# The weights of an input projection: eleven more units split into two matmul parts, with all thirteen low parts of that pass made by GpSimd

## The reference

```
mod = silu(c) @ w_ada + b_ada                     # six vectors per sequence
h = rmsnorm(x) * (1 + sc1) + sh1
proj = h @ w_in                                   # 1024 -> 2176 columns: 17 units of 128
ya = pool_mixer(proj[..., :256]);  yb = conformer_conv(proj[..., 256:1024]);  yc = short_conv(proj[..., 1024:])
x = x + gt1 * rmsnorm(concat(ya, yb, yc) @ w_out)
h = rmsnorm(x) * (1 + sc2) + sh2
x = x + gt2 * rmsnorm((silu(h @ w_gate) * (h @ w_up)) @ w_down)
```

## Time and profile before

| | |
|---|---|
| median of 3 runs | 2261.96 us (2261.28 to 2262.41) |
| profiled execution, its own time | 2261.27 us |
| its span | 2259.5 us |
| granted TensorE clock, mean | 0.999 |
| busy: PE, DVE, ACT, POOL | 2244.3, 1343.5, 1001.7, 38.1 us |

### The profile page before, as it was taken

One profiled execution on the slowest core, in us unless ns is written; L12 is line 12 of the kernel. 1 busy time (PEld: TensorE's weight loads), 2 busy tenths in 40 slices (PEclk: granted clock), 3 DMA queues, 4 the chain that ended last, 5 costly groups with the idle time before them and its releaser, 6 DMA issues.

```text
span 2259.5 us, 29953 instructions
## 1 busy us (share of the span) xinstructions
PE 2244.3 (99%) x12270; PEld 2069.7 (92%) x12270; DVE 1343.5 (59%) x1957; ACT 1001.7 (44%) x1408; POOL 38.1 (2%) x83
## 2 busy tenths in 40 slices
PE   9999999999999999999999999999999999999998
PEld 6779998979999988999898899989899998899987
DVE  3779866698444577653467855357784435443343
ACT  3455466454444534353544435354443425432332
POOL 0000000000000000000000000000000000000000
PEclk9999999999999999999999999999999999999999
DMA  9864653544443533544353353435335434444332
GB/s 376 309 221 164 242 200 137 177 168 169 167 151 129 183 125 123 185 149 156 125 185 123 126 210 122 156 124 186 122 128 180 123 130 153 155 149 159 123 129 94
DMA packets 103046, 368.98 MB, mean 163 GB/s; under 512 B 12631, under 2 KB 14807, under 8 KB 102396
## 3 DMA queue, kind: packets, MB, share of 16 engines
q1 hardware_dynamic: 102910, 367.06, 45.8%
HBM read 348.02 MB, written 19.00 MB: 162 GB/s over the span
## 4 chain that ended last, share of the span: by engine, by line
PE 91%; DVE 4%; ACT 0%; issue 0%; DMA 0%; DVEq 0%; ACTq 0%
PE ps L636 90%; DVE wlo L1349 1%; DVE pr L1500 1%; PE ps L706 1%; DVE early L1500 0%; PE ps L666 0%; DVE g_lo L1401 0%; DMA raw<-in_w_mix 0%; DVE h_lo L1394 0%; ACT h_f L1035 0%; ACT junk L990 0%; DVE pr L1522 0%; DVE h_wait L1378 0%; ACT whi L967 0%; DVE h_wait L1380 0%
## 5 line engine op out<-in xcount | busy, mean ns | idle before, releaser
L1349 DVE TENSOR_TENSOR wlo<-raw,whi 128x1024 fp32r<-128x1024 f32 x531 | 646.7, 1221 | 525.6 <-ACT whi L967 524.1
L636 PE MATMUL ps<-h_hi,whi 128*128 128x384 f32 (+1 forms) x2808 | 923.9, 329 | 1.9 <-DVE h_lo L1394 1.1
L967 ACT ACTIVATE whi<-raw 128x1024 fp32r<-128x1024 f32 x531 | 561.1, 1058 | 817.8 <-DMA raw<-in_w_gu 536.9
L636 PE MATMUL ps<-h_hi,wlo 128*128 128x384 f32 (+1 forms) x2808 | 919.4, 327 | 0.0
L636 PE MATMUL ps<-h_lo,whi 128*128 128x384 f32 (+1 forms) x2808 | 919.2, 327 | 0.0
L636 PEld LDWEIGHTS ps<-h_hi,whi 128*128 128x128 f32 x2808 | 528.6, 188 | 8.4 <-issue 4.8
L636 PEld LDWEIGHTS ps<-h_lo,whi 128*128 128x128 f32 x2808 | 528.6, 188 | 1.8
L636 PEld LDWEIGHTS ps<-h_hi,wlo 128*128 128x128 f32 x2808 | 528.6, 188 | 0.0
L636 PE MATMUL ps<-whi,g_hi 128*128 128x512 f32 x748 | 235.1, 395 | 1.7 <-issue 0.9
L636 PE MATMUL ps<-whi,g_lo 128*128 128x512 f32 x748 | 231.1, 390 | 0.0
L636 PE MATMUL ps<-wlo,g_hi 128*128 128x512 f32 x748 | 230.8, 390 | 0.0
(11 more groups left out here) (143 smaller groups left out, 1303.7 us busy)
## 6 DMA issues: line engine op xcount, KB each, us to landing
raw<-in_w_gu SPq DMA_DIRECT2D x264, 512.0 KB, 3.2
raw<-in_w_mix SPq DMA_DIRECT2D x150, 512.0 KB, 3.2
raw<-in_w_dn SPq DMA_DIRECT2D x132, 512.0 KB, 3.2
xr<-in_x_all SPq DMA_DIRECT2D x29, 512.0 KB, 5.9
xr<-x_all SPq DMA_DIRECT2D x17, 512.0 KB, 5.9
pre<-in_w_ada SPq DMA_DIRECT2D x16, 512.0 KB, 10.4
x_all<-xr SPq DMA_DIRECT2D x5, 1536.0 KB, 7.3
xr<-in_w_ada SPq DMA_DIRECT2D x12, 512.0 KB, 7.4
```

The costliest lines, as they stand in the source:

```text
L636: return nc.tensor.matmul(out, lhsT, rhs, start=start, stop=stop, skip_group_check=True)
L967: nc.scalar.activation(whi[:, s, :], raw[:, s, :], ACT.Copy).then_inc(w_hi, 1)
L1349: tt(wlo[:, s, :], raw[:, s, :], whi[:, s, :].bitcast(F32), ALU.subtract).then_inc(w_lo, 1)
```

## The change

Units 4 to 16 are now all split. Eleven units, 6 to 16, go from 8 plain float32 matmuls to 24 faster ones and need a `high` on ScalarE and a low part each. All thirteen low parts of the first projection, those of units 4 and 5 too, are made by GpSimd (`first_low`) and counted by a semaphore of their own, `w_lo_pool`. VectorE makes the low parts from unit 17 on, as before. GpSimd's norm root for block 1 is put ahead of the low part of unit 15.

```
-PARTS0, PARTS1 = 4, RING
+PARTS0 = 4
 def whole(n):
-    return n < PARTS0 or PARTS1 <= n < NIN
+    return n < PARTS0
 def splits(n):
-    return sum(not whole(i) for i in range(n + 1))
+    return max(0, n + 1 - PARTS0)
+def vec_lows(n):
+    return n + 1 - NIN
             def wait_split(n):
-                pe.wait_ge(w_lo, splits(n))
+                pe.wait_ge(*((w_lo_pool, splits(n)) if n < NIN else (w_lo, vec_lows(n))))
             for j in range(PARTS0, NIN):
-                if whole(UNIT["in", 0, j]):
-                    project_whole(j)
-                else:
-                    project(0, j)
+                project(0, j)
+            def first_low(n):
+                s = n % RING
+                pool.wait_ge(w_hi, splits(n))
+                nc.gpsimd.tensor_tensor(wlo[:, s, :], raw[:, s, :], whi[:, s, :].bitcast(F32), ALU.subtract)\
+                    .then_inc(w_lo_pool, 1)
             x_rstds("M", 0)
-            x_rstds("M", 1)
+            for n in range(PARTS0, NIN):
+                if n == NIN - 2:
+                    x_rstds("M", 1)
+                first_low(n)
             def ahead(*key):                      # VectorE's
                 n = UNIT[key] + LEAD
-                if n < TOTAL and not whole(n):
+                if NIN <= n < TOTAL:
                     low(n)
-            low(PARTS0)
             h_rest(0, KD - 2)
             h_rest(0, KD - 1)
-            for n in range(PARTS0 + 1, RING):
-                low(n)
```

More of the change, by code:

```diff
@@ L333, in build @@
         w_lo = sem("w_lo")
+        w_lo_pool = sem("w_lo_pool")
         w_used = sem("w_used")
@@ L728, in by_columns @@
                 last.then_inc(w_used, 1)
-            def project_whole(j):
-                pe.wait_ge(evac_done, evac_count(0, j - 2))
-                first_unit(j, range(KD))
             def first_unit(j, ks):
```

## The result

The changed kernel takes 2276.3 us in the median of 4 runs (2275.1 to 2278.1) against 2262.0 us (2261.3 to 2262.4, 4 runs): +14.3 us, ratio 1.0064 with a 95% interval of 1.0051 to 1.0077. It is slower, 1.7 us above the forecast and inside its range. The profiled execution took 2275.1 us, its span is 2273.3 us and the mean granted clock 0.995.

The account below looks back on a forecast made before the run. TensorE, busy 2244.3 of 2259.5 us, was taken as the bound. VectorE's delay of +17.0 less 3.7 for modulation columns gave +13.3 on 2261.3 us: 2274.6 us, range 2269.6 to 2279.6, with the clock 2282.

Parts of the forecast that it names:

- VectorE's path: From VectorE's mixing to unit 17's transposes: GpSimd's low parts keep VectorE out, so the transposes start 13.3 us later.
- ScalarE's order: First projection: high parts waiting for loads hold up evacuations in ScalarE's queue, eating TensorE's saved 6.7 us; net +2.4 us.
- Rival B: VectorE isn't kept out, or too little; only TensorE's path counts, +2.4 us, 2263.7 us; chance 22%.
- Kept out for the whole of each low part: VectorE's work beside units 6 to 16: each GpSimd low part costs it 2.3 us with the handover, 25.3 us in all.
- GpSimd's low part: Duration of one 128 x 1024 subtraction on GpSimd in the first projection: 2.25 us, the middle of 1.8 and 2.7.
- +17.0: VectorE's delay before the first h_rest of block 1: 25.3 us kept out, less the wait of 8.31 us.
- -3.7: Modulation columns on TensorE, 3.71 us between first h_rest and last transposes, would be done in the wait instead.
- 0 to 3 us: Left out of the sum: a longer low-clock spell on TensorE after unit 16 could add this much.
- +13.3 predicted: Later start of the transposes before unit 17, 17.0 - 3.7 us, which nothing further on returns.
- TensorE's path: First projection on TensorE, saving and ScalarE's waits counted: ends at 96.6 instead of 94.2 us, +2.4, hidden below VectorE's path.
- The other is let in between two: Engine sharing, VectorE and GpSimd: an instruction holds what both need to its end, then the other engine gets in.
- rival D: GpSimd is kept out for good while VectorE has steady work, delaying low part 6 to 74.5 us: 2279 us; chance 7%.

## Why the prediction was right, and where it was off

- **VectorE's path decides, not TensorE's.** Shown by the chain, by TensorE's 6.70 us wait, and by the runs: without the reads the time falls by 9.8 us, with VectorE making the low parts itself by 8, while ScalarE's order, worth 3.9 us without them, is worth nothing that shows with them. Rival B is out.
- **Kept out for the whole of each low part**, 11 x 2.3 = 25.3 us. Measured: the own low part starts 15.7 us late and 8.3 us of wait are gone, 24.0 us; 0.65 of it is a later start of the mixing (45.29 instead of 44.64 us). So 23.4 us over eleven low parts, 2.1 each: nine lengthened taps and two lengthened copies. This direction was a choice between nothing and all, since no row of before showed it; the row above of 56.47, a tap that ends with GpSimd's low part, shows that "all" is nearly right. For the shorter subtractions it is less so (1.1 of 1.5 us).
- **The rule of the Trainium skill** that I weighed there (SBUF — State Buffer, "Who interferes with whom"), that the two engines lock each other out for the whole instruction, agrees with the trace in both directions (a tap went from 0.48 to 2.63 us, and GpSimd's low part of unit 15 from 2.34 to 7.34). The same section counts copies and tensor_scalar among the instructions that can take what both share; the trace agrees (0.23 to 2.31 us, and 0.41 to 2.50). Its other half, that whoever issues first goes first, does not cover the low parts that were held off while tap after tap was issued behind them.
- **GpSimd's low part**, 2.25 us taken: 2.34 us when alone, 2.57 in the median. Right.
- **+17.0 became +15.7**, the first h_rest came at 112.8 instead of 114, since a low part took 2.1 and not 2.3 us.
- **-3.7 became -2.2.** The columns were indeed done in the wait. But from the 15.7 us of VectorE to the 13.56 by which the last transposes are late (120.82 - 107.26) only 2.2 us are gained. The modulation product ahead of these transposes took 3.57 us (117.25 to 120.82); before it took 2.8 (104.45 to 107.26). Two stretches of the kernel after (columns as in the earlier trace rows, the granted clock is the third number from the end):

```profile
104.00:112.00 8.00, 3.48 (x17) 3.38 (x16) 8.00 (x20) 0.00 (x0) 0.00 (x0) 0.50 0.46 162
116.00:120.00 4.00, 3.79 (x20) 1.09 (x19) 3.40 (x10) 3.05 (x6) 0.00 (x0) 0.50 0.00 0
```

  At 0.50, that is 1.2 GHz, in both stretches, where the earlier trace rows had 0.50 for the two microseconds from 104. This is what the prediction left out of its sum as 0 to 3 us. I read some 0.8 us from the product (it takes 3.57 us in the kernel without the reads too); no run isolates it. The rest, some 0.7 us, is a size: from the first h_rest to the last transposes it was 10.17 us before (97.09 to 107.26) and is 8.01 now (112.81 to 120.82), 7.2 with a product of 2.8, so the columns had stood in the way for only 2.9 of their 3.71 us. The two errors, 1.3 and 1.5 us, cancel nearly: +13.3 predicted, +13.56 measured. That it came so close is luck; the terms themselves are right to some 1.5 us.
- **TensorE's path**: unit 9 starts at 69.6 (69.4), the evacuation of unit 11 ends at 83.61 (83.1), the end of unit 16 is 3.3 us later (+2.4). The mechanism is right and hidden, and by itself, in the kernel without the reads, it is worth +4.0 us. That is more than rival B's price of 2.4, and not because TensorE needs it: the chain of that kernel goes through VectorE. What is late is ScalarE's high part of unit 17, behind the other high parts, the evacuations and the scalings; VectorE waits 12.60 us for it (8.31 in the earlier trace rows), and from there low parts, taps and h_rest follow one another on the chain until the transposes. The prediction hadn't followed this branch of the late order.
- **"The other is let in between two" failed.** One instruction of GpSimd was held off in four kernels: it took 7.3 and 12.9 us in the changed one, 12.95 in the one with the reads alone, 18.8 with the swapped order, and 16.9 and 17.1 with the added matmuls. It was let in at a copy behind the train of taps each time. So rival D's mechanism exists and came in an irregular part, against the 7% that the prediction gave it. Its price did not come in the two profiles of the changed kernel: VectorE goes undisturbed meanwhile and pays afterwards, and the chain stays with VectorE. It did come where something waited for the instruction that was held off: the norm root behind it in the kernel with the reads alone, TensorE with the swapped order. Why GpSimd is let in between some pairs of taps and not between others stays open, and so does why it goes otherwise in two executions of the same program.

## What to carry to other kernels

An idle engine is not free if it reads SBUF too: beside a float32 VectorE stream, each GpSimd instruction with SBUF inputs cost VectorE most of its own duration here (2.1 of 2.3 us, 1.1 of 1.5), and the question is then whether VectorE would do the work faster (1.14 against 2.1 us here). Place such work where VectorE waits (no gain is shown for that here, and no loss), or give GpSimd only writes, which cost no time here. Keep what others wait for, such as a norm root, ahead of such an instruction: it may be held off for over 10 us. And when high parts, loads and evacuations share one queue in order, put the evacuation that others wait for ahead of the instruction that waits for a load, but expect nothing from it until it is on the path.

## What the runs showed of the hardware

- GpSimd's instruction of 2.3 us can be held off for 5 to 16 us more by a train of VectorE's taps of 0.4 us, and which instruction it hits differs between executions of one program, with the medians of the changed kernel's two measurements within 0.1 us of each other (2276.3 and 2276.4).
- VectorE's one-input float32 copies and scalings are shut out as well (0.19 us became 2.41, 0.41 became 2.50), while 28 memsets of GpSimd in the same places cost at most 0.5 us in a few of them and nothing in the time.
- A GpSimd memset of 128 x 1024 float32 takes 0.95 us (in the kernel without the reads), the subtraction of the same size 2.34.
- TensorE's clock can take back what was gained ahead of it: the same modulation columns took 3.71 us at a granted clock of 1.00 and 5.39 at 0.52, and two whole units that took 7.17 us before took 8.86 behind a wait of 3.67 us, with the clock at 0.50 for a part of them.
